# Using raw keys and queries in the gated DeltaNet part of a hybrid encoder block

## What is computed

```python
qkv = silu(causal_depthwise_conv(concat([q, k, v]), conv_w))
q = l2norm(q) * 128 ** -0.5          # l2norm(t) = t * rsqrt(sum(t * t) + 1e-6)
k = l2norm(k)
beta = sigmoid(beta_logit)
g = -exp(a_log) * softplus(a_logit + dt_bias)
G = cumsum(g)                        # in a chunk
decay = exp(G[:, None] - G[None, :]) # lower triangle
A = strict(k @ k.T * decay * beta[:, None])
# (I + A) is inverted; rhs is v * beta and k * beta * exp(G)
qk = (q @ k.T) * decay
# over the chunks, with the state S:
#   v_new = u - w @ S;  o = (q * exp(G)) @ S + qk @ v_new
#   S = S * exp(G_last) + (k * exp(G_last - G)).T @ v_new
o = rmsnorm(o, out_norm) * silu(z)   # per head
```

## Time and profile before

| | us |
|---|---|
| median of 3 runs | 3272.18 (3269.68 to 3272.93) |
| the profiled execution | 3265.26 |
| its span, first to last instruction | 3263.7 |
| PE busy | 2990.4 (92%) |
| DVE busy | 2590.6 (79%) |
| ACT busy | 1997.9 (61%) |
| POOL busy | 949.3 (29%) |

### The profile page before, as it was taken

The page is one execution under the profiler, slowest core; times in us unless marked ns, Lnnn a source line. Parts: engine busy times, 40 slices in busy tenths (PEclk is TensorE's granted clock), DMA queues, the critical chain, the costliest instruction groups (busy, mean ns, idle before and its releaser), DMA issues. The chain is left out here.

```text
span 3263.7 us, 81939 instructions
## 1 busy us (share of the span) xinstructions
PE 2990.4 (92%) x28778; PEld 2233.3 (68%) x28779; DVE 2590.6 (79%) x7206; ACT 1997.9 (61%) x4412; POOL 949.3 (29%) x994
## 2 busy tenths in 40 slices
PE   3777999999999999999999999997699999999970
PEld 3766878888887888788878888885344555555430
DVE  6878778887887888788878887886788888888755
ACT  4555566666665656565666666653577777777646
POOL 4313122212221222132222212221344444544420
PEclk9889999999999999999999999998899999999985
DMA  7010111211212111212111111214387877677749
GB/s 264 27 53 14 47 66 65 67 66 66 72 63 76 60 67 66 73 60 73 66 66 65 68 66 66 72 56 200 118 255 222 243 202 214 187 219 216 220 99 394
DMA packets 117811, 380.30 MB, mean 117 GB/s; under 512 B 18560, under 2 KB 18688, under 8 KB 105216
## 3 DMA queue, kind: packets, MB, share of 16 engines
q1 hardware_dynamic: 82528, 269.96, 22.6%
q0 software_dynamic: 29216, 89.30, 11.9%
q10 hardware_dynamic: 5760, 16.85, 1.3%
HBM read 280.05 MB, written 96.01 MB: 115 GB/s over the span
## 5 line engine op out<-in xcount | busy, mean ns | idle before, releaser
L578 PE MATMUL pj<-uT,W 128*128 128x128 f16 x15840 | 982.9, 220 | 0.0
L578 PEld LDWEIGHTS pj<-uT,W 128*128 128x128 f16 x15840 | 936.8, 98 | 45.7 <-issue 37.6
L2038 DVE SCALAR_TENSOR_TENSOR W<-W,ecol 128x512 f16<-128x512 f16 x664 | 447.6, 747 | 111.9 <-ACT W L1982 107.4
L1982 ACT ACTIVATE W<-W,ecol 128x512 f16 x664 | 416.2, 710 | 79.7 <-issue 77.2
L1946 PE MATMUL bA<-W,uT 128*128 128x512 f16 x1992 | 446.6, 381 | 5.4 <-issue 4.1
L1946 PEld LDWEIGHTS bA<-W,uT 128*128 128x128 f16 x1992 | 193.5, 98 | 228.6 <-issue 9.1
L1741 POOL TENSOR_TENSOR dec<-tri,g 128x512 f32<-128x512 f32 x33 | 34.4, 1042 | 925.6 <-DVE g L1461 925.6
L1930 PE MATMUL pj<-W,qs 128*128 x664 | 301.8, 598 | 1.9 <-issue 1.0
L917 ACT ACTIVATE ht<-ht 128x512 f32<-128x512 f32 x256 | 159.9, 627 | 94.6 <-DMA ht<-w_up 90.2
L1930 PEld LDWEIGHTS pj<-W,qs 128*128 128x128 f32 x664 | 120.9, 192 | 123.3 <-issue 122.9
L947 ACT ACTIVATE qh<-bA 128x256 f32<-128x256 f32 x198 | 76.8, 388 | 193.4 <-PE bA L678 188.1
(11 more groups left out here) (444 smaller groups left out, 6310.0 us busy)
## 6 DMA issues: line engine op xcount, KB each, us to landing
ht<-w_gate SPq DMA_DIRECT2D x128, 256.0 KB, 3.2
ht<-w_up SPq DMA_DIRECT2D x128, 256.0 KB, 3.4
W<-w_gate SPq DMA_DIRECT2D x32, 1024.0 KB
W<-w_up SPq DMA_DIRECT2D x32, 1024.0 KB
W<-w_down SPq DMA_DIRECT2D x32, 1024.0 KB
x_in<-xm SPq DMA_DIRECT2D x33, 512.0 KB, 4.5
ht<-xm SPq DMA_DIRECT2D x32, 512.0 KB, 3.5
h_rows<-ht SPq DMA_DIRECT2D x32, 512.0 KB
```

The source lines that it names most:

```text
L578: mm = pe.matmul(pj[g % 2][:, j, :], w16[:, k, w_half(w_high, COL[GROUPS[g]], 512, j * P, P)], (ul if low_u else uh)[:, k, :], start=(k == ...
L1982: nc.scalar.activation(part_of(wx[par][:, 0], k), raw[:, k], ACT.Copy, scale=ecol[par][:, k:k + 1]).then_inc(sem("wx_high"), 1)
L2038: a = nc.vector.scalar_tensor_tensor(out=part_of(wx[par][:, 1], k), in0=raw[:, k], scalar=ecol[par][:, k:k + 1], in1=part_of(wx[par][:, 0] ...
```

## The change

Keys and queries are no longer normalized. `ks` and `qs` enter all products raw, and the norms are put in elsewhere:

- The two products with ones and the transposes of L763 go. In their place, at the end of a step, PE transposes the raw keys into `bB` and the raw queries into `bA`, eight 128x128 transposes.
- ACT sums the squares of each head over the free axis (four functions with an accumulator for keys, four for queries), and copies the transposed keys to `kd`. DVE then multiplies `kd` by its decay in place, from SBUF.
- The key's norm goes into `beta` (divided by the squared norm: `eb` is multiplied by `ssk`) and into `vt` (four copies scaled by `rn`, in place of one copy). The query's norm cancels in the output's RMS norm but for its epsilon, which `qe` holds: four logarithms with a bias each in place of one.
- The softplus on ACT and its products on DVE move from the head of a step to the end of the step before. Of `beta` only the addition moves with them; the reciprocal and the negation stay, behind the new factor.
- The copies to `vt` move ahead of the residual's squares on ACT.
- The squares of keys and queries on ACT and the multiplications L1470 and L1473 on DVE go.

```diff
@@ PE, stage s.G
-                        need(pe, sem("unit_ready"), 2 * s.pG + 1)
                         need(pe, sem("nq_used"), s.nG)
                         for h in range(H):
-                            mm = pe.matmul(bA[:, h, :], kh[:, h, :], kh[:, h, :], start=True, stop=True)
+                            mm = pe.matmul(bA[:, h, :], ks[:, h, :], ks[:, h, :], start=True, stop=True)
...
-                        need(pe, sem("M_raw"), 2 * s.nG)
-                        for h in range(H):
-                            mm = pe.transpose(bT[:, h, :], kh[:, h, :], ident[:])
-                        mm.then_inc(sem("pre_full"), 1)
@@ PE, end of the step
-                        need(pe, sem("sq_k"), s.nP)
+                        need(pe, sem("qkv_silu"), 3 * s.pP + 2)
                         need(pe, sem("al_ready"), s.nP)
-                        pe.matmul(flat(bB), ones[:], flat(kh), start=True, stop=True).then_inc(sem("nk_full"), 1)
-                        need(pe, sem("sq_q"), s.nP)
+                        for h in range(H):
+                            mm = pe.transpose(bB[:, h, :], ks[:, h, :], ident[:])
+                        mm.then_inc(sem("nk_full"), 1)
                         need(pe, sem("lrs_ln"), s.nG)
-                        pe.matmul(flat(bA), ones[:], flat(rnq), start=True, stop=True).then_inc(sem("nq_full"), 1)
+                        for h in range(H):
+                            mm = pe.transpose(bA[:, h, :], qs[:, h, :], ident[:])
+                        mm.then_inc(sem("nq_full"), 1)
@@ ACT, head of the step
...
                         need(act, sem("nk_full"), s.nG)
-                        rsqrt(bB[:], kh[:], 1.0, eps[:], ("nk_used", s.nG), "rk_ready")
-                        need(act, sem("nq_full"), s.nG)
-                        rsqrt(bA[:], rnq[:], 1.0, eps[:], ("nq_used", s.nG), "rq_ready")
+                        for h in range(H):
+                            nc.scalar.activation(junk[:, h * P:h * P + P], bB[:, h, :], ACT.Square, accum_out=ssk[:, h:h + 1])
...
+                        nc.scalar.activation(kd[:], bB[:], ACT.Copy).then_inc(sem("nk_used"), 1)
+                        need(act, sem("nk_used"), s.nG)
+                        nc.scalar.activation(rn[:], ssk[:], ACT.Ln, bias=eps[:]).then_inc(sem("rn_step"), 1)
...
+                        need(act, sem("nq_full"), s.nG)
+                        for h in range(H):
+                            a = nc.scalar.activation(junk[:, 512 + h * P:512 + h * P + P], bA[:, h, :], ACT.Square, accum_out=ssq[:, h:h + 1])
+                        a.then_inc(sem("nq_used"), 1)
...
+                        for h in range(H):
+                            a = nc.scalar.activation(vt[:, h, :], bC[:, h, :], ACT.Copy, scale=rn[:, h:h + 1])
+                        a.then_inc(sem("vt_ready"), 1)
@@ ACT, end of the step
-                        rsqrt(oss[:], ors[:], 1.0 / P, eps[:], ("o_ln", s.nG), "o_norm")
+                        for h in range(H):
+                            a = nc.scalar.activation(ors[:, h:h + 1], oss[:, h:h + 1], ACT.Ln, scale=1.0 / P, bias=qe[:, h:h + 1])
+                        a.then_inc(sem("o_ln"), 1)
+                        need(act, sem("o_ln"), s.nG)
+                        nc.scalar.activation(ors[:], ors[:], ACT.Exp, scale=-0.5).then_inc(sem("o_norm"), 1)
@@ DVE, head of the step
-                        need(dve, sem("b_exp"), s.nG)
-                        nc.vector.tensor_scalar(eb[:], eb[:], 1.0, None, ALU.add).then_inc(sem("b_step"), 1)
-                        need(dve, sem("b_step"), 2 * s.pG + 1)
+                        need(dve, sem("b_step"), 3 * s.pG + 1)
+                        need(dve, sem("nk_used"), s.nG)
+                        nc.vector.scalar_tensor_tensor(out=eb[:], in0=ssk[:], scalar=EPS, in1=eb[:], op0=ALU.add,
+                                                       op1=ALU.mult).then_inc(sem("b_step"), 1)
+                        need(dve, sem("b_step"), 3 * s.pG + 2)
                         nc.vector.reciprocal(beta[:], eb[:]).then_inc(sem("b_step"), 1)
...
-                        nc.vector.tensor_tensor(kh[:], ks[:], kh[:], ALU.mult).then_inc(sem("unit_ready"), 1)
...
-                        nc.vector.scalar_tensor_tensor(out=qh[:], in0=qs[:], scalar=P ** -0.5, in1=rnq[:], op0=ALU.mult,
-                                                       op1=ALU.mult).then_inc(sem("unit_ready"), 1)
@@ DVE, ahead of Mt
+                        need(dve, sem("nq_used"), s.nG)
+                        need(dve, sem("o_norm"), s.pG)
+                        nc.vector.tensor_scalar(qe[:], ssq[:], P * EPS, P * EPS * EPS, ALU.mult, ALU.add)
@@ DVE, behind ot
-                        nc.vector.tensor_tensor(kd[:], bT[:], rows(ekd[:]), ALU.mult).then_inc(sem("kd_ready"), 1)
+                        nc.vector.tensor_tensor(kd[:], kd[:], rows(ekd[:]), ALU.mult).then_inc(sem("kd_ready"), 1)
```

More of the change, by code:

```diff
@@ L263, in hymba_block @@
         ors = sb("ors", [P, H])
+        ssk = sb("ssk", [P, H])
+        ssq = sb("ssq", [P, H])
+        rn = sb("rn", [P, H])
+        qe = sb("qe", [P, H])
         aahh = sb("aahh", [P, 8, P])
@@ L655, in turn_delta @@
                     need(pe, sem("yt_ready"), s.nO)
-                    need(pe, sem("kd_ready"), s.nG)
                     for h in range(H):
@@ L1008, in body @@
                     if s.G:
-                        need(act, sem("pre_full"), 5 * s.pG + 3)
-                        need(act, sem("vn_full"), s.pG)
-                        nc.scalar.activation(vt[:], bC[:], ACT.Copy).then_inc(sem("vt_ready"), 1)
                         need(act, sem("w_ready"), s.nG)
@@ L1090, in body @@
                         nc.scalar.activation(qs[:], qs[:], ACT.Silu).then_inc(sem("qkv_silu"), 1)
-                        need(act, sem("qkv_silu"), 3 * s.pP + 1)
-                        need(act, sem("kS_full"), s.nG)
-                        if isinstance(s.i, int) and s.nP == 1:
-                            act.wait_ge(sem("w_split"), len(GROUPS))
-                        nc.scalar.activation(kh[:], ks[:], ACT.Square).then_inc(sem("sq_k"), 1)
                     if s.G:
@@ L1107, in body @@
                         nc.scalar.activation(zs[:], pj[1][:], ACT.Silu, scale=dsc[:, 5:6]).then_inc(sem("z_done"), 1)
-                        need(act, sem("qkv_silu"), 3 * s.pP + 2)
-                        need(act, sem("Su_full"), s.nG)
-                        nc.scalar.activation(rnq[:], qs[:], ACT.Square).then_inc(sem("sq_q"), 1)
                     if s.G:
@@ L1117, in body @@
                         nc.scalar.preload_act_table_set("natural_log_exp_and_others")
+                        need(act, sem("al_ready"), s.nP)
+                        need(act, sem("g_step"), 2 * s.nG)
+                        nc.scalar.activation(ga[:], al[:], ACT.Abs).then_inc(sem("g_ln"), 1)
+                        need(act, sem("beta_ready"), s.nG)
+                        nc.scalar.activation(eb[:], sgb[:], ACT.Exp, scale=-1.0).then_inc(sem("b_exp"), 1)
+                        need(act, sem("g_ln"), 3 * s.pP + 1)
+                        nc.scalar.activation(ga[:], ga[:], ACT.Exp, scale=-1.0).then_inc(sem("g_ln"), 1)
+                    for h in range(H):
+                        if s.G:
+                            if h == 0:
+                                need(act, sem("o_ready"), s.nG)
+                            a = nc.scalar.activation(junk[:, h * P:h * P + P], ot[:, h, :], ACT.Square, accum_out=oss[:, h:h + 1])
+                            if h == H - 1:
+                                a.then_inc(sem("o_ss"), 1)
+                        if s.P and h == 0:
+                            need(act, sem("g_ln"), 3 * s.pP + 2)
+                            nc.scalar.activation(ga[:], ga[:], ACT.Ln, bias=1.0).then_inc(sem("g_ln"), 1)
                     if s.G:
-                        need(act, sem("o_ready"), s.nG)
-                        for h in range(H):
-                            a = nc.scalar.activation(junk[:, h * P:h * P + P], ot[:, h, :], ACT.Square, accum_out=oss[:, h:h + 1])
-                        a.then_inc(sem("o_ss"), 1)
                         need(act, sem("lnorm_full"), s.nG)
@@ L1508, in body @@
                                                        op1=ALU.mult).then_inc(sem("w_ready"), 1)
-                        need(dve, sem("pre_full"), 5 * s.pG + 4)
+                        need(dve, sem("pre_full"), 4 * s.nG)
                         need(dve, sem("M_raw"), 2 * s.pG + 1)
@@ L1629, in body @@
                     conv(s, 3, vs, 0, 1, 2, 3)
+                    if s.P:
+                        need(dve, sem("g_ln"), 3 * s.nP)
+                        need(dve, sem("grow_full"), s.nG)
+                        nc.vector.scalar_tensor_tensor(out=g4[:], in0=al[:], scalar=0.0, in1=ga[:], op0=ALU.max,
+                                                       op1=ALU.add).then_inc(sem("g_step"), 1)
+                        need(dve, sem("g_step"), 2 * s.pP + 1)
```

(3 more changed lines are left out.)

47 lines of the change are left out of this document (16 added, 31 removed).

## The result

| | before | after |
|---|---|---|
| median, us | 3270.53 (3263.66 to 3272.93, 11 runs) | 3283.44 (3275.03 to 3289.41, 11 runs) |
| the profiled execution, us | 3265.26 | 3286.22 |
| its span, us | 3263.7 | 3284.6 |
| PE, DVE busy, us | 2990.4, 2590.6 | 2966.0, 2582.4 |
| ACT, POOL busy, us | 1997.9, 949.3 | 2008.6, 931.1 |

The ratio of the times is 1.0041 (95% interval 1.0032 to 1.005): slower by 12.9 us. That is slower, as forecast, but by a third of the 39 us; 3283.44 lies in the range (3244 to 3334) and outside the likeliest case's own (3295 to 3330).

What follows compares the result with a forecast made beforehand. PE bounds the kernel, busy 1923.59 of 1932 us; it loses 1.28 us of work a step, but POOL holding DVE delays `Mt`, so a step gains 1.25; times 31 is 39, giving 3311 us, 8-in-10 range 3244 to 3334.

Steps and rivals of the forecast that it cites:

- the likeliest case's own: Whole kernel: range of 3295 to 3330 us for the case that two holds slow each step; chance 0.66.
- the sentence on L720: PE, head of step: L720 doesn't wait, since `g4` and POOL's L1741 (1.04 us) run in the step before.
- a square with its accumulator takes 0.31: ACT, squares of keys ahead of the betas: 0.31 us each, four 1.24, so `nk_used` comes at 1260.48.
- the two holds: DVE, four rows of `yt`: POOL's L1748 and L1749 each hold one row, 1.04 us each, 2.08 together.
- X's copy (1.07): POOL, filling X: held by the clamp, runs 1.07 us from 1262.35 to 1263.4 and holds `ekd` to 1263.3.
- the 0.2 for `kd` and `qe`: DVE: `kd` from two SBUF inputs may be held by POOL; with `qe`'s possible wait, 0.2 us a step added.
- the paragraph on other edits: DVE and ACT, later in the step: `kd` held nothing to 1 us, mostly hidden by PE's projections; `vt` nearly free.
- The residual's squares behind `vt` wait for a late `residual` in any case: ACT, `vt` copied ahead of the residual's squares: the squares wait for a late `residual` anyway; no cost added.
- the holds don't come: First rival, DVE's `yt` rows: no holds, rows end by 1263.3, gain 1.0 us a step, 3241 us; chance 0.20.
- One hold as before: Rival, DVE's `yt` rows: L1749 gets no turn between them, rows end at 1265.6, no change, 3272 us; chance 0.08.
- More holds: Rival, DVE: `qe` and `kd` also wait for a whole POOL operation each, 2.5 us more a step, 3350; chance 0.06.
- What would show it: Signs in the profile: clamp about 0.8, `yt` rows over 3 us, PE idle some 2 us before `Mt`'s transposes, step 65.2 to 66.2.

Runs made afterwards that it cites:

- e9: Changed kernel with the decay's four small ACT functions and DVE's three products for `g4` and `eb` back at the head of the step; 3299.32 us, 65.57 a step.
- e1: Changed kernel with POOL's filling of X moved ahead of its product with `nbeta`; 3277.6 us, ratio to before 1.0029, step 64.73.
- e2: Changed kernel with DVE's betas waiting for the four squares of keys alone, not for the copy to `kd`; 3278.84 us, step 64.73.
- e8: Changed kernel with only ACT's residual squares put back ahead of `vt`; 3279.24 us, ratio to before 1.0035, step 64.89.
- e5: e1 plus ACT's residual squares back ahead of the copies to `vt`; 3242.55 us, ratio to before 0.9923, step 63.65.
- e3: Changed kernel with POOL's second product (`dec` by the triangle) waiting for the four rows of `yt`; 3274.2 us, ratio to before 1.0016, step 64.73.
- e11: Control: kernel before the change, with POOL's filling of X ahead of its product with `nbeta`; 3283.08 us, ratio to before 1.0034, step 64.97.
- e6: e1 plus DVE's product for `kd` moved behind the levels, ahead of `vn`; 3259.85 us, ratio to before 0.9976, step 64.22.
- e7: e5 plus DVE's `kd` product moved behind the levels, as in e6; 3237.99 us, ratio to before 0.9911, step 63.51.
- e10: Kernel before the change, with only `vt` copied ahead of the residual's squares on ACT; 3275.53 us, ratio to before 1.0015, step 64.59.

## Why the prediction was right in sign and three times too large

**PE's own work** was right: 1.1 us a step less by the windows, against 1.28 (some records of matmuls can be missing). L734 began at 7.37 behind the transposes, the 7.37 forecast; e9 shows 0.84 of it to hang on the move of the decay, as the sentence on L720 assumed.

**ACT.** The squares began at 1258.57 on the forecast's clock, against 1258.61: the four small functions cost 0.45 and the three more logarithms 0.56, as taken (0.45 and 0.57). The term "a square with its accumulator takes 0.31" was too large: they stand 0.25 apart, read from PSUM, and the copy took 0.61 and not 0.63. `kd` was copied at 1260.18, not at 1260.48, and `nbeta` began at 1260.69 and not at 1260.95. 1260.18 lies 0.02 outside the bounds given (1260.2 to 1260.75).

**POOL and the two holds.** The mechanism was right in each part that was named: the clamp 0.70 (0.75 forecast), the held `ekd` (0.56; "about a microsecond" was too much), two rows of `yt` held. The step that failed in size is "X's copy (1.07)". That row of before was itself a held operation; DVE ran `qh` beside it (to 1261.90; the copy 1261.30 to 1262.37):

```profile
1260.89 1.01 DVE L1473 SCALAR_TENSOR_TENSOR qh<-qs,rnq 128x512 f32<-128x512 f32 x1 [0.43 <-ACT rnq L931]
```

Alone, the copy takes 0.61 (e1, e2); behind the clamp it took 0.81 and ended at 1262.73 instead of 1263.4. So the rows began 0.7 earlier than forecast, and `residual` was late by 0.71 and not by 1.45. Of the 0.7, 0.26 is ACT's, and the other 0.4 is the copy: a wait and a full 1.07 had been summed where it took 0.81 in all. With the 0.2 for `kd` and `qe`, below, less the 0.1 by which L681 followed `Mt` later than forecast, this makes up about the 0.8 a step by which the forecast was too high. Everything behind moves with it:

| | forecast | measured, same clock |
|---|---|---|
| `residual` | +1.45 | +0.71 |
| `Mt` begins | 1268.1 | 1267.38 |
| transposes of `Mt` | 1268.85, PE 2.0 behind | 1268.21, PE 1.35 behind |
| first L681 | 1274.1, +1.05 | 1273.49, +0.44 |
| step | +1.25 | +0.45 |

Two slips of the forecast's sum are smaller: 1266.6 less 1265.19 is 1.41 and not 1.45, and from the transposes of `Mt` PE would reach L678 at 1273.76 (5.35 less 0.44 behind 1268.85) and not at 1273.65, which `ot` hides. The forecast added 0.2 for `kd` and `qe` to the 1.05; nothing of it came to this chain. `kd` took 0.96 and not 0.69, but PE had projections to do, as the paragraph on other edits said. The bound of 0.8 to 1.8 a step was too tight, since it had been built on the held row and on 0.2 that isn't there.

**What the prediction missed altogether** is the second chain. "The residual's squares behind `vt` wait for a late `residual` in any case" holds only as long as the first chain is there: `residual` ends at 1278.23, 0.17 after `vt` began, and e8, with the squares first, gains nothing (64.89). Once `residual` is in time, the squares could fill ACT's 2.75 us of waiting and don't; in e5 they do, and `vt` isn't later. That this didn't spoil the forecast of the time is luck: its 64.73 hides just below the 64.87 of the first chain. Had the holds not come, the same working would have said 63.4, and the step would have been 64.73 (e2). But it makes the first rival wrong as well: *the holds don't come*, priced at 63.4 a step and 3241, is what e2 realizes by its own condition (betas 0.49 earlier, one held row), and e2 takes 3278.84. The rival's price would have been right only with the squares in their old place (e5: 3242.55). *One hold as before* is e3: the rows took 2.15 as described, and its 3272 was near e3's 3274.2, but by the other chain, not by `Mt`. *More holds* didn't come in the sense meant, but `kd` is held more wherever the first chain is loosened (1.65 in e1 and e2, 1.33 in e3).

Of "What would show it", the clamp, the rows over 3 us and PE's wait ahead of the transposes of `Mt`, released by DVE, came, and none of the signs of being wrong. The wait was 1.18 in the profile (1.35 by the starts) and the step 64.87, below the 65.2 to 66.2. The copy to `kd` ended 2.97 behind the transposes, not 3.3.

What stays open: 6.6 us of the 20.9 between the two profiled executions lie ahead of the first key transposes (137.6 and 140.9 us into the span) and behind the last ones (1041.0 and 1044.3 us). No run was aimed at them, but over the profiles of all versions these stretches range from 137.6 to 140.9 and from 1035.7 to 1046.9 whatever the edit, and the medians differ by 12.9, about what the steps account for (14).

## What to carry to other kernels

When a change takes work from the engine that bounds a kernel, write down every chain that ends within a microsecond of its waits, not only the one that becomes the bound: here two stood 0.14 apart, each edit that removed one brought at most 0.14 us a step, and the pair brought 1.22, some 40 us in all. Before a row of the trace is used as a price, see what ran beside it; a duration that contains a hold is no price for the same instruction elsewhere. In an engine's queue put ahead of a wait what is ready by then, and where an operand moves from PSUM to SBUF ask what GpSimd runs at that time.

## What the runs showed of the hardware

- POOL's 128x512 copy takes 0.61 us where no DVE instruction holds it (e1, e2), 0.81 with DVE's clamp beside it, 1.07 and 1.15 (e11) with larger DVE instructions.
- A DVE product with two SBUF inputs of 128x512 (`kd`) takes 0.69 with POOL quiet (e6, e7), 0.96 to 1.65 beside POOL, and 0.68 with one of the inputs in PSUM, beside `gx` (e10). The Trainium skill (SBUF — State Buffer, Who interferes with whom) says that a DVE instruction with at most one SBUF input, outside the two-port modes, doesn't contend; the 0.68 agrees.
- The taps `xc` of L1169, each a scalar operation from SBUF to SBUF with columns from SBUF, are held as well: four take 1.11 unhindered, 1.66 beside `zg` (e1, e10) and 2.73 beside `gx` and `zg` (e6). The same section of the Trainium skill (SBUF — State Buffer, Who interferes with whom) excepts the two-port modes from that sentence and names the scalar operation as one that can enter them, as the forecast had it for SBUF to SBUF. The holds agree with this; whether it is such a mode or the columns was not tried.
- A hold by `zg` doesn't last to the end of `zg`. In the changed kernel `kd` (1284.26 to 1285.22) lies inside it as far as POOL's recorded span goes, so the forecast's "whoever issues second blocks fully" fits POOL's products beside `yt`, but not this row:

```profile
1283.99 1.57 POOL L1784 TENSOR_SCALAR zg<-zs,sd 128x512 f32<-128x512 f32 x1
```

- Squares of 128x128 with an accumulator stand 0.25 us apart on ACT from PSUM. From SBUF the first two stand 0.31 apart and the others 0.29 to 0.30, in the changed kernel 0.29; the forecast's 0.31 was the longest of them.
